# Hybrid attention and convolution block on eight cores: later key and query weights and tiles, reordered group ends, halved last blocks

## The reference

```python
h = rms_norm(x, g_pre)
q, k, v, z_a, cb, cc, cx, z_c, ga, gc = split(h @ w_in)
lam = exp(sum(lq1 * lk1)) - exp(sum(lq2 * lk2)) + lam_init
s = q @ k.T * 64 ** -0.5 - slope[head] * distance
p = softmax(causal(s))
o = rms_norm((p[map 0] - lam * p[map 1]) @ v, subln_gain) * (1 - lam_init)
y_attn = (o * silu(z_a)) @ w_attn_o
u = causal_depthwise_conv(cc * cx, conv_w)
y_conv = ((cb * u) * silu(z_c)) @ w_conv_o
y = sigmoid(ga + b_a) * y_attn + sigmoid(gc + b_c) * y_conv
out = x + rms_norm(y @ w_out, g_post)
```

## Time and profile before

| | us |
|---|---|
| median of 3 runs | 779.58 (777.16 to 779.83) |
| the profiled execution, its own time | 780.28 |
| its span on the slowest core, core 4 | 778.7 |
| spans of the other cores | 772.3 to 778.1 |
| first scores of attention | 156.5 |
| start of the merge | 547.2 |
| start of the output projection | 713.2 |

### The profile page before, as it was taken

One profiled execution on the slowest core, in us unless ns is written; L12 is line 12 of the kernel. 1 busy time (PEld: TensorE's weight loads), 2 busy tenths in 40 slices (PEclk: granted clock), 3 DMA queues, 4 the chain that ended last, 5 costly groups with the idle time before them and its releaser, 6 DMA issues.

```text
span 778.7 us, 15293 instructions; the slowest of 8 cores (772.3 to 778.7 us)
## 1 busy us (share of the span) xinstructions
PE 724.1 (93%) x5370; PEld 382.2 (49%) x5370; DVE 368.8 (47%) x829; ACT 377.5 (48%) x552; POOL 152.5 (20%) x165
## 2 busy tenths in 40 slices
PE   4799999998888998799999999899999999999995
PEld 1354444455555454455555556555444444444442
DVE  3666444222654456657565467746522222222444
ACT  2446555264565654376666667675222222223433
POOL 1100000105711000010100001101333332321663
PEclk9999999998999999899999999999999999999998
DMA  7997973810000110000100101002852222200786
GB/s 166 246 209 203 252 168 68 128 22 2 2 2 29 28 18 12 2 15 15 29 2 2 28 2 28 3 1 56 134 123 41 41 42 40 42 1 1 247 293 221
DMA packets 39684, 57.68 MB, mean 74 GB/s; under 512 B 23825, under 2 KB 24209, under 8 KB 39346
## 3 DMA queue, kind: packets, MB, share of 16 engines
q1 hardware_dynamic: 31682, 39.58, 18.4%
q0 software_dynamic: 7776, 16.78, 13.8%
q10 hardware_dynamic: 144, 0.26, 0.1%
HBM read 59.76 MB, written 8.39 MB: 88 GB/s over the span
## 4 chain that ended last, share of the span: by engine, by line
PE 84%; DVE 7%; issue 4%; ACT 2%; DMA 1%; DVEq 0%; POOL 0%; SPq 0%; ACTq 0%; POOLq 0%
PE psum L1428 14%; PE psum L823 13%; PE psum L1159 12%; PE psum L725 11%; PE psum L711 8%; PE psum L1481 7%; PE psum L1435 7%; PE psum L1099 6%; PE psum L858 4%; ACT arena L1128 2%; DVE arena L1199 1%; PE psum L688 1%; DVE arena L1204 1%; PE psum L1239 1%; DMA arena<-gpre 1%
## 5 line engine op out<-in xcount | busy, mean ns | idle before, releaser
L1128 ACT ACTIVATE arena<-psum 128x1024 bf16<-128x1024 f32 (+2 forms) x259 | 219.0, 902 | 112.5 <-PE psum L1099 111.9
L1159 PE MATMUL psum<-arena 128*128 128x130 bf16 x1780 | 134.0, 223 | 5.3 <-DVE arena L1199 2.8
L1159 PEld LDWEIGHTS psum<-arena 128*128 128x128 bf16 x1780 | 106.0, 99 | 54.2 <-issue 47.9
L823 PE MATMUL psum<-arena 128*128 128x512 bf16 x512 | 126.3, 389 | 5.7 <-DVE arena L1186 2.1
L1428 PE MATMUL psum<-arena 128*128 128x512 bf16 x512 | 115.7, 379 | 0.0
L1440 ACT ACTIVATE arena<-psum,arena 128x512 f32<-128x512 f32 x64 | 44.0, 687 | 120.4 <-PE psum L1428 120.4
L1444 DVE SCALAR_TENSOR_TENSOR arena<-arena,psum 128x512 f32<-128x512 f32 x64 | 43.8, 687 | 115.8 <-PE psum L1435 115.8
L725 PE MATMUL psum<-arena 128*128 128x512 bf16 x384 | 88.4, 379 | 0.0
L1099 PE MATMUL psum<-arena 64*128 64x512 bf16 (+3 forms) x568 | 73.8, 340 | 6.3 <-ACT arena L1128 3.9
L1428 PEld LDWEIGHTS psum<-arena 128*128 128x128 bf16 x512 | 50.1, 98 | 60.2
L823 PEld LDWEIGHTS psum<-arena 128*128 128x128 bf16 x512 | 47.6, 99 | 54.9 <-issue 12.6
(11 more groups left out here) (101 smaller groups left out, 626.3 us busy)
## 6 DMA issues: line engine op xcount, KB each, us to landing
arena<-x_perm SPq DMA_DIRECT2D x48, 512.0 KB, 6.4
arena<-w_chunk POOLq DMA_DIRECT2D x40, 256.0 KB, 4.8
out_own<-arena SPq DMA_DIRECT2D x15, 512.0 KB, 4.7
arena<-w_y POOLq DMA_DIRECT2D x8, 256.0 KB, 5.5
arena<-wo_r POOLq DMA_DIRECT2D x1, 2048.0 KB, 20.6
arena<-w_wide POOLq DMA_DIRECT2D x4, 256.0 KB, 11.4
arena<-w_wide POOLq DMA_DIRECT2D x1, 1024.0 KB, 11.9
arena<-gpost SPq DMA_DIRECT2D x1, 512.0 KB, 3.6
```

What stands on the lines that cost most here:

```text
L823: p.op("pe", (lambda e: e.matmul(bank(bk), lhsT=lhs(kc), rhs=rhs(kc), start=(kc == 0), stop=(kc == n - 1))), reads=rd, writes=[("bank", bk)])
L1128: p.op("act", (lambda e, a0=a0, a1=a1, c0=c0, c1=c1, bias=bias: e.activation(out=PT[sl][:, a0:a1, c0 * 128:c1 * 128], in_=psum[:, a0:a1, c ...
L1159: p.op("pe", (lambda e, kd=kd, m=m, cb=cb, acc=acc, first=first, vj=vj: e.matmul(acc, lhsT=PT[sl][:, 2 * kd + m, cb * 128:(cb + 1) * 128], ...
```

## The change

It is made of these parts.

- `key_loads`: the loads of the key weights are issued at block 1 and wait for x blocks 6 to 9; the query weights wait for blocks 9 to 12.
- The quota of key and query tiles is 0 up to block 7, then 2 per own block and 1.34 per partner block.
- The squares of the norm check run on ACT in place of POOL. The call for every unit ahead of the fork is gone, so all of them are issued in the loop at the unit before `FORK`. Norm tiles may finish out of order.
- Three buffers `sz` in place of two. A group's z tile goes to the front of the filler at the group's first unit. The forced transposes at the start of `epilogue` are gone; a gate waits for the transposes of two groups before instead.
- Tiles carry what they need (`need`); `next_ready` lets the first tile without a need go ahead when the front tile's need is later than TensorE's clock. `put_fill` stops whenever bank 7 is not free within 0.15 us.
- The last two output blocks, not only the last, run by halves.

```diff
+            NZ = 3
+            sz_at = [sz_off, sz_off + 2 * K, take(2 * K)]
+            sz = [reg(a, 2 * K, F32).rearrange("p (b n) -> p b n", b=4) for a in sz_at]
...
-            for h in range(4):
-                w_part(wk[h], w_chunk[4 + h].rearrange("p (a b) -> p a b", a=KC), ("wk", h), f"ldwk{h}", (xld[2 + h],))
+            def key_loads():
+                for h in range(4):
+                    w_part(wk[h], w_chunk[4 + h].rearrange("p (a b) -> p a b", a=KC), ("wk", h), f"ldwk{h}", (xld[6 + h],))
...
-                    w_part(wq[h], w_chunk[h].rearrange("p (a b) -> p a b", a=KC), ("wq", h), f"ldwq{h}", (xld[6 + h],))
+                    w_part(wq[h], w_chunk[h].rearrange("p (a b) -> p a b", a=KC), ("wq", h), f"ldwq{h}", (xld[9 + h],))
...
+                if n == 1:
+                    key_loads()
...
-                quota += 0.0 if n < 4 or kd == 2 else 1.0 if kd == 1 else 2.0
+                quota += 0.0 if n < 8 or kd == 2 else 1.34 if kd == 1 else 2.0
...
-                tb = g % 2
+                tb = g % NZ
...
-                while pieces and not kq_left and pieces[0][0] < 2 + len(normed) and p.now["pool"] < until:
+                while pieces and not kq_left and (pieces[0][0] < 2 or pieces[0][0] - 2 in normed) and p.now["act"] < until:
...
-                    p.op("pool", (lambda e, i=i, t=t, src=src: e.tensor_tensor(out=sq[i % 2][:, t * 512:(t + 1) * 512], in0=src, in1=src, op=ALU.mult)),
-                         reads=[name], writes=[("sq", i % 2, t)], t=1.35)
+                    p.op("act", (lambda e, i=i, t=t, src=src: e.activation(out=sq[i % 2][:, t * 512:(t + 1) * 512], in_=src, func=AF.Square)),
+                         reads=[name], writes=[("sq", i % 2, t)], t=0.58)
...
-                    if i == len(NORMS) - 1:
+                    if len(normed) == len(NORMS):
...
             def epilogue(s, h, g):
                 ob = g % 2
-                while g >= 2 and g - 2 not in t_done:
-                    fill.step()
...
-                    while g not in z_done:
+                    while g not in z_done or (g >= 2 and g - 2 not in t_done):
                         fill.step()
...
-                    tile_ = {"mm": mm, "post": post, "n": 4, "w": 0.057}
+                    tile_ = {"mm": mm, "post": post, "n": 4, "w": 0.057, "need": [("gat", ob, qb) for qb in range(4)]}
...
+            def next_ready():
+
+                if p.when(fill.q[0].get("need", [])) > now["pe"] + 0.1:
+                    later = [k for k, t in enumerate(fill.q) if "need" not in t]
+                    if later:
+                        fill.q.insert(0, fill.q.pop(later[0]))
...
-                    if not fill.open:
-
-                        free = p.unread(("bank", 7))
-                        if hot or (free > now["pe"] + 0.15 and free + 0.2 > until):
-                            break
+                    if not fill.open and (hot or p.unread(("bank", 7)) > now["pe"] + 0.15):
+                        break
                     if fill.left() <= TAIL:
                         break
+                    if not fill.open:
+                        next_ready()
                     one()
...
                     if g:
-                        z_wait = (s, h, g)
+                        fill.push(z_tile(s, h, g))
...
-                if z_wait and not any(x[0] <= g - 2 for x in side):
-                    fill.push(z_tile(*z_wait))
-                    z_wait = None
...
                 elif n < FORK:
-                    squares_of(now["pe"] + 0.6)
                     if way:
                         load_way()
...
-                if n == NB - 1:
+                if n >= NB - 2:
                     last_block(n, i, b, b0)
                     return
...
-                eng = "dve" if n >= NB - 2 else "pool"
-                p.op(eng, (lambda e: e.tensor_tensor(out=ostage[b], in0=ostage[b], in1=xres[b], op=ALU.add)),
+                p.op("pool", (lambda e: e.tensor_tensor(out=ostage[b], in0=ostage[b], in1=xres[b], op=ALU.add)),
```

More of the change, by code:

```diff
@@ L409, in emission @@
             sz_off = take(4 * K)
-            sz = [reg(sz_off + i * 2 * K, 2 * K, F32).rearrange("p (b n) -> p b n", b=4) for i in range(2)]
             gc_off = take(16 * K)
@@ L485, in emission @@
                 p.place(("zr", i), zr_off[i], 2 * K)
-                p.place(("sz", i), sz_off + i * 2 * K, 2 * K)
             p.place(("wz",), wz_off, 8 * K)
@@ L491, in emission @@
             p.place(("tz",), tz_off, 2 * K)
+            for i in range(NZ):
+                p.place(("sz", i), sz_at[i], 2 * K)
             for i in range(NR):
@@ L924, in post @@
                         fill.q.insert(min(1, len(fill.q)), way_tile())
-                return {"mm": mm, "post": post, "n": 16, "w": 0.057}
+                return {"mm": mm, "post": post, "n": 16, "w": 0.057, "need": [("sq", i % 2, t) for t in range(4)]}
             def way_tile():
@@ L1256, in epilogue @@
                 for qb in range(4):
-                    side.append((g, 0.35, lambda qb=qb: gate(qb), [("rs", ob), ("sz", ob), ("z", g)]))
+                    side.append((g, 0.35, lambda qb=qb: gate(qb), [("rs", ob), ("sz", g % NZ), ("z", g)]))
                 side.append((g, 0.0, trans, []))
@@ L1264, in open_z @@
             def open_z(names):
-                return all(n[1] in z_done and not hot and not any(n in c_[0] for c_ in chain) for n in names if n[0] == "z")
+                return all(n[1] in z_done and (n[1] < 2 or n[1] - 2 in t_done) and not hot and not any(n in c_[0] for c_ in chain)
+                           for n in names if n[0] == "z")
             LEAD = 0.12
@@ L1514, in last_block @@
                     p.op("act", (lambda e, half=half: e.activation(out=junkf[:, cols[half]], in_=bank(b0 + half), func=AF.Square,
-                                                                   accum_out=ssf[:, n + half:n + half + 1])),
-                         reads=[("bank", b0 + half)], writes=[("ssh", half), ("junkf",)])
+                                                                   accum_out=ssf[:, 2 * n - 14 + half:2 * n - 13 + half])),
+                         reads=[("bank", b0 + half)], writes=[("ssh", n, half), ("junkf",)])
                     p.op("dve", (lambda e, half=half: e.tensor_tensor(out=ostage[b][:, cols[half]], in0=bank(b0 + half), in1=gpost[:, cols[half]],
                                                                       op=ALU.mult)),
-                         reads=[("bank", b0 + half), ("gpost",)], writes=[("osh", half), ("ost", b)])
-                p.op("dve", (lambda e: e.tensor_tensor(out=ssf[:, n:n + 1], in0=ssf[:, n:n + 1], in1=ssf[:, n + 1:n + 2], op=ALU.add)),
-                     reads=[("ssh", 0), ("ssh", 1)], writes=[("ssf", n)])
+                         reads=[("bank", b0 + half), ("gpost",)], writes=[("osh", n, half), ("ost", b)])
+                p.op("dve", (lambda e: e.tensor_tensor(out=ssf[:, n:n + 1], in0=ssf[:, 2 * n - 14:2 * n - 13], in1=ssf[:, 2 * n - 13:2 * n - 12], op=ALU.add)),
+                     reads=[("ssh", n, 0), ("ssh", n, 1)], writes=[("ssf", n)])
                 root(n)
```

13 lines of the change are left out of this document (6 added, 7 removed).

## The result

The changed kernel takes **818.49 us** (median of 4 runs, 817.05 to 819.5) against 779.38 for the kernel before: ratio 1.0506 [1.0478, 1.0534], 39.1 us slower. The forecast was 779.5 us (771 to 788). The profiled execution is 817.05 us, its slowest core is core 0.

What follows compares the result with a forecast made beforehand. TensorE, busy 93% of the span, was taken as the bound. Terms +5.0 + 4.0 - 8.1 - 1.0 + 0 = -0.1 us on the profiled 780.28 us, with the median 0.7 lower, gave 779.5 us (771 to 788).

Steps and rivals of the forecast that it cites:

- Start, +5.0: First blocks: four key tiles leave blocks 4 to 7 and come back where TensorE is full; net +5.0 us (+4 to +6).
- rival (c): Start costs nothing: x blocks land earlier without key weights beside them, first blocks come closer; 774.5 us, chance 0.06.
- Other group ends, -1 (-5 to +4): Group ends besides fifth and sixth: waits of 0.4 to 0.8 us each, against filling that stops earlier; -1 us.
- Norm check, +4.0 (-1 to +11): 180 to 280 us: -14.7 us from what goes, +18.7 us for the loop ahead of the fork; together +4.0 us.
- Rival (b): Loop ahead of the fork: rounds at half clock, 7 us each, groups behind start cold; 786 us, chance 0.29.
- the 23.6 of the sum: Loop ahead of the fork: three rounds of 6.0 us, one conv tile with eviction and the check, 23.6 us in all.
- Fifth and sixth end, -8.1: Group ends at 299 and 315 us: epilogue begins earlier, a conv tile fills TensorE's gap; gain 3.6 + 4.5 us.
- Rival (a): Group ends give all: fifth and sixth lose nothing (-11), the others give 5; 772.5 us, chance 0.24.
- The same wait under another name: Group ends: sign that the prediction is wrong, TensorE's wait for line 872 there returning under another name.
- Last two blocks, 0: End of program: block 14 by halves, last steps begin at about 773.5 in place of 773.61; 0 (-0.7 to +0.7) us.

Runs made afterwards that it cites:

- the kernel with the loop alone: Kernel before with the norm check's squares on ACT, all in the loop ahead of the fork, norm tiles in the changed order: 794.94 us, ratio 1.02.
- the kernel with both edits: Changed kernel with the old stop rule of put_fill and the squares called at every unit on ACT again: 781.23 us, ratio 1.0014.
- the reordered ends alone: Kernel before with the reordered group ends and squares on ACT unit by unit; old filling rule, start and last blocks: 773.08 us, ratio 0.994.

## Why the prediction was wrong

- **Start, +5.0: right.** +4.0 alone. The steps of 3.43 us are there, and the wait for VectorE, not for x, decides, so rival (c) falls. Block 8 starts at 43.71 and not near 45.8 because the first blocks ran 2 us earlier on this core (block 3 at 26.56, for 28.60); from block 3 to the first scores it is 133.1 us for 127.9, 5.2 more.
- **Other group ends, -1 (-5 to +4): the step that failed most.** The words were "filling now stops whenever the spare bank is not free, where it waited before", and the term was sized by the waits at group ends. The rule runs in every unit. By the old rule TensorE waited for bank 7 when it came free within the unit's time, and went on filling until the exponentials were due; now the planner goes on to the scores, and TensorE waits there for ACT, up to 1.8 us, unfilled. Measured: +12.8 us by itself, +26 beside the loop. The step that was left out was to count how often the old rule waited, by the units and not by the ends.
- **Norm check, +4.0 (-1 to +11): mis-sized in three terms, the one behind the loop by far the most.** Take the kernel with the loop alone (+15.6 us) and a conv tile at 1.73 us. Ahead of the loop it is 10.6 us shorter (110.7 for 121.3) with five tiles more in it, so 19.2 us were won and not 14.7. The loop took 26.9 us and not 23.6. Behind it the stretch is 1.6 us longer (264.1 for 262.5) with eight tiles fewer in it, so 15.4 us were lost, where the sum has 2 us of slow clock. Together -4.5 + 3.3 + 13.4 = 12.2 us above the 4.0; measured 11.6 above. What the 15.4 us are is in part open. The granted clock of that stretch is 0.95 for 0.98, and it is below full in all four rows from 280 to 360 us. But at the sixth group end TensorE also waits 4.0 us for an eviction behind the gates (3.57 for line 872 before), and with more tiles done early there were fewer left to fill with. Nor is it a fixed price: in the changed kernel with the old rule the loop takes the same 26.7 us, but by the same count only 5.6 us are lost behind it, against the kernel with both edits.
- **Rival (b)** had the right sign and place, and its tiles at half clock are there: 3.17, 3.50 and 3.30 us for tiles of 1.89, behind waits of 0.3 to 1.8 us. The Trainium skill (TensorE: Matmul & The Clock Gate, "HAM oscillation") describes a loop of short matmul bursts and waits, there for a DMA, in which every turn starts at the slow clock; these rows agree with it. The point from which it was to decide, a round over 6.5 us, was hardly reached: two rounds measured 5.4 and 6.2 (5.4 and 6.7 with the loop alone). The whole loop, 25.9 and 26.9 us, lies between the 23.6 of the sum and the 28.5 of this rival. The loss lay less in the rounds than behind them.
- **Fifth and sixth end, -8.1: failed.** The sum let VectorE's epilogue begin right behind the gates, and so it does. It then let the next accumulation wait only 1.1 and 1.9 us for its banks, with the gates at their old time. But the gates wait for POOL's root, and the change leaves what leads to it in place: the waits are 3.02 and 4.10 us in the changed kernel, 0.96 and 3.16 with the reordered ends alone. Rival (a) falls with it. "The same wait under another name" was listed as what would show it wrong, and line 1203 is it. With the root issued one unit earlier the longest wait for the epilogue went from 3.2 us to 1.0, and the kernel gained some 2.7 us and not 8: a stall that goes at one place was booked as time of the whole kernel, and where the rest is lost no run shows.
- **Last two blocks, 0: +1.6.** The multiplications were laid beside ACT's squares. `op` orders two engines that read the same bank, so they come one behind the other, in block 14 (0.49 us of waiting) as in block 15.
- **Left open.** The parts by themselves, 4.0 + 15.6 + 0.1 + 12.8 + 1.6, make 34 of the 39 us. The parts do not add: the rule costs 26 us where the loop is in and some 16 where it is not, and the loop, against squares by unit, 22 alone, 20.8 beside the new rule and 11.1 beside the old rule and the reordered ends. Why, no run shows. Of the 26 us behind the fork on core 4 I don't know what is rule, what is clock and what are the group ends.

## What to carry to other kernels

A rule that says when filler work stops is priced by how often it is asked, not at the place where it was put in for. Work that is spread thin beside a full TensorE is cheap (24 squares on ACT: 5.5 us gained against POOL); the same work in one block cost its length (27 us with four filling tiles in it) and 6 to 15 us more behind it. When a stretch gets shorter or longer, count the filling tiles in it before you call that a gain or a loss. Before a stall is booked as a gain, read down the in-order queue of the engine that frees the buffer: what stands ahead there is the next name of the wait.

## What was not expected of the hardware

The squares on POOL slowed VectorE, and only some of its operations. These are groups of instructions from 175 to 245 us (busy us, mean ns of one, idle time before), first of the kernel before:

```profile
L1140 DVE TENSOR_TENSOR arena<-arena 128x512 bf16<-128x512 bf16 x4 | 3.3, 814 | 0.7 <-ACT arena L1128 0.7
L994 DVE TENSOR_SCALAR arena<-arena 128x512 f32<-128x512 f32 x2 | 2.5, 1258 | 0.0
...
L980 DVE COPY arena<-psum 128x512 f32<-128x512 f32 x3 | 2.1, 687 | 7.7 <-PE psum L823 7.7
```

And of the kernel with the squares on ACT:

```profile
L1140 DVE TENSOR_TENSOR arena<-arena 128x512 bf16<-128x512 bf16 x5 | 2.1, 420 | 0.6 <-ACT arena L1128 0.6
L994 DVE TENSOR_SCALAR arena<-arena 128x512 f32<-128x512 f32 x3 | 1.4, 481 | 0.0
...
L980 DVE COPY arena<-psum 128x512 f32<-128x512 f32 x3 | 2.1, 692 | 8.5 <-PE psum L823 8.5
```

The mask (line 1140) and the scaling (line 994), whose operands all lie in SBUF, go from 814 to 420 ns and from 1258 to 481; the eviction from PSUM (line 980) takes 0.69 us in both. From 340 to 540 us, where POOL has no squares, the kernel before takes 421 and 478 ns for the first two. The Trainium skill (SBUF — State Buffer, "Who interferes with whom") says that VectorE and GpSimd take turns at one shared pair of ports, which VectorE needs for two SBUF inputs or its two-port modes; these rows agree for the mask, which has two SBUF inputs; which mode the scaling runs in they do not show. The granted clock of 180 to 200 us, 0.83 before, is 1.00 in the second kernel. The squares themselves took 1.15 us each on POOL and take 0.53 in the bursts on ACT, with no load of a table ahead of them, as the prediction assumed. The one load of a table there, 1.28 us ahead of the first exponentials behind the fork, is in the kernel before too.
